# A hybrid RWKV-7, Mamba-2 and PEER step on one core: modulation products in two-part fp32r with 18 stationary columns, a halved last inverse level, weight splits ahead of stores, an unrolled TensorE program

## The reference, cut to what matters

```python
def _layer(x, c, shift0, wkv0, conv0, ssm0, lp):
    mod = jax.nn.silu(c) @ lp['w_ada'] + lp['b_ada']        # c: 9 conditioning rows; 6 x 1024 columns
    sh1, sc1, gt1, sh2, sc2, gt2 = jnp.split(mod, 6, axis=-1)
    xn = _rmsnorm(x, lp['norm1_g']) * (1 + sc1[:, None]) + sh1[:, None]
    proj = xn @ lp['w_in']                                  # 50 tiles of 128 columns, and 16 columns for dt
    p_rw, p_ssm, p_gate = ...
    o_a, wkvT = _rwkv7(p_rw, ...)                           # gate g, decay w, a: products of low rank, then the state
    o_b, convT, ssmT = _mamba2(p_ssm, ...)                  # x, B, C through a convolution of 4 taps and silu
    x = x + gt1[:, None] * (merged @ lp['w_out'])
    xn2 = _rmsnorm(x, lp['norm2_g']) * (1 + sc2[:, None]) + sh2[:, None]
    x = x + gt2[:, None] * _peer(xn2, ...)                  # 8 heads, top 16 of 128 x 128 experts per token
```

## Time and profile before

| | |
|---|---|
| median of 3 runs | 4652.97 us (4641.38 to 4659.5) |
| the profiled execution's own time | 4650.29 us |
| its span | 4648.5 us |
| PE busy | 4303.7 us (93%) |
| DVE busy | 3202.1 us (69%) |
| ACT busy | 1439.4 us (31%) |
| POOL busy | 1349.9 us (29%) |
| mean granted TensorE clock | 0.954 of full |

### The profile page before, as it was taken

One profiled execution on the slowest core, in us unless ns is written; L12 is line 12 of the kernel. 1 busy time (PEld: TensorE's weight loads), 2 busy tenths in 40 slices (PEclk: granted clock), 3 DMA queues, 4 the chain that ended last, 5 costly groups with the idle time before them and its releaser, 6 DMA issues. The chain is left out here.

```text
span 4648.5 us, 86226 instructions
## 1 busy us (share of the span) xinstructions
PE 4303.7 (93%) x32847; PEld 3863.9 (83%) x32847; DVE 3202.1 (69%) x6005; ACT 1439.4 (31%) x2182; POOL 1349.9 (29%) x1059
## 2 busy tenths in 40 slices
PE   6999998999767897999998999799999999999997
PEld 3888887777654786978887888799999999999997
DVE  4731332444384324889995555699999999999997
ACT  2211221111154322223335666322222222222223
POOL 5333222000002220024443222344344343434341
PEclk8999999999786998999999999899999999999999
DMA  4555555445262331124443455799999999999994
GB/s 158 184 185 191 187 191 181 171 162 204 74 190 78 106 122 56 37 68 144 143 143 135 162 180 183 273 303 303 299 302 299 302 300 300 300 299 305 297 302 165
DMA packets 522992, 927.81 MB, mean 200 GB/s; under 512 B 284032, under 2 KB 351232, under 8 KB 518688
## 3 DMA queue, kind: packets, MB, share of 16 engines
q1 hardware_dynamic: 380448, 547.61, 36.1%
q0 software_dynamic: 80960, 346.96, 21.9%
q10 hardware_dynamic: 61392, 30.52, 2.2%
HBM read 785.79 MB, written 206.30 MB: 213 GB/s over the span
## 5 line engine op out<-in xcount | busy, mean ns | idle before, releaser
L3188 POOL DMA_INDIRECT ex_rows<-expert_rows,ex_here x512 | 587.3, 1147 | 952.2 <-DVE acc_tok L3323 861.0
L3323 DVE SCALAR_TENSOR_TENSOR acc_tok<-ex_rows,ex_wsp,acc_tok 128x1024 f32<-128x1024 f32 x512 | 633.5, 1278 | 0.0
L2586 PE MATMUL ex_psa<-x_dense_high,eg_u_high 128*128 128x288 f32 x2048 | 604.4, 295 | 15.3 <-DVEq L3377 13.9
L2586 PE MATMUL ex_psa<-x_dense_low,eg_u_high 128*128 128x288 f32 x2048 | 604.6, 295 | 0.0
L2586 PE MATMUL ex_psa<-x_dense_high,eg_u_low 128*128 128x288 f32 x2048 | 604.2, 295 | 0.0
L2677 POOL TENSOR_TENSOR eg_u_low<-eg_u,eg_u_high 128x1024 fp32r<-128x1024 f32 x130 | 326.7, 2513 | 844.1 <-ACT eg_u_high L2672 844.1
L3220 PE MATMUL ex_pso<-ex_w_high,ex_v_high 128*128 128x288 f32 x2048 | 441.4, 297 | 8.9 <-DVE acc L3305 6.1
L3220 PE MATMUL ex_pso<-ex_w_high,ex_v_low 128*128 128x288 f32 x2048 | 440.1, 297 | 0.0
L3220 PE MATMUL ex_pso<-ex_w_low,ex_v_high 128*128 128x288 f32 x2048 | 439.1, 296 | 0.0
L3251 ACT ACTIVATE ex_w<-ex_psa 128x288 f32<-128x288 f32 x256 | 105.4, 412 | 1059.6 <-PE ex_psa L2586 1038.8
L3305 DVE TENSOR_TENSOR acc<-ex_pso,acc 128x576 f32<-128x576 f32 x512 | 373.7, 750 | 47.2 <-PE ex_pso L3220 47.2
(11 more groups left out here) (521 smaller groups left out, 9442.3 us busy)
## 6 DMA issues: line engine op xcount, KB each, us to landing
eg_u<-in_u SPq DMA_DIRECT2D x256, 512.0 KB, 3.7
expert_rows<-in_v SPq DMA_DIRECT2D x128, 512.0 KB, 6.1
ex_v<-in_v SPq DMA_DIRECT2D x128, 512.0 KB
weights<-wt_stage SPq DMA_DIRECT2D x9, 4096.0 KB, 12.1
ex_g<-weights SPq DMA_DIRECT2D x128, 288.0 KB
expert_rows<-eg_act SPq DMA_DIRECT2D x256, 128.0 KB, 1.7
proj<-in_out POOLq DMA_DIRECT2D x50, 548.5 KB, 3.3
in_w<-in_w_in SPq DMA_DIRECT2D x50, 512.0 KB, 3.6
```

What stands on the lines that cost most here:

```text
L2586: yield nc.tensor.matmul(out[:, 0:b - a], w[:, kc, :], half[:, kc, a:b], start=n == 0, stop=n == len(passes) - 1)
L3188: pool.indirect_dma_start(rows[i][:, :], None, table, index(here[par][:, t, j:j + 1]), element_offset=ROW_RUNS[t][0]).then_inc(s_row[i], 16)
L3323: v.scalar_tensor_tensor(out=acc_tok[:, t, :], in0=rows[i][:, at:at + D], scalar=wsp[:, i:i + 1], in1=acc_tok[:, t, :], op0=ALU.mult, op1= ...
```

## The change

It has six parts.

1. POOL splits the 16 dt columns of w_in first (`first_split`), and clears old semaphores (`clear_retired`) at the end of its program for the inputs.
2. In the inputs loop POOL waits for tile t's matmuls and splits the weights of tile t + 2; the store of tile t, which waits for the evacuation, comes behind.
3. In the four RWKV rounds the gate product and its copy come first, then zw, za, norm, bonus.
4. The last inverse level computes only the half that is used: PE leaves out one of the two matmuls, and DVE's `t` and `xy` are 128x256 in place of 128x512.
5. In rw_prompt POOL splits each 128x3072 chunk of w_ada (CAST, TENSOR_TENSOR), and the condition into 18 columns (high and low side by side). PE runs 16 fp32r matmuls in place of 8 of fp32; the row has 18 partitions, and the product that turns it adds its two halves (`fold`).
6. PE's program in spread is in line.

```diff
+    def first_split(self, pool):
+        pool.wait_ge(self.s_wdt, 16)
+        self.split(pool, self.wdt, self.wdth, self.wdtl, 0)
...
-                k.clear_retired()
+                pj.first_split(pool)
...
                 t = 2 * r + parity
+                pool.wait_ge(self.s_mm, t + 1)
+                split(t + 2, parity, r + 1)
                 store(t, parity)
-                split(t + 2, parity, r + 1)
...
-                            product(lw[0:64, r, 0, :], lora[0:64, 0, :], "zw")
+                            product(lw[:, r, 1, :], lora[:, 1, :], "gate")
                         elif j == 1:
+                            pe.wait_ge(AC.sem, AC.now("gate", r))
+                            product(lw[0:64, r, 0, :], lora[0:64, 0, :], "zw")
+                        elif j == 2:
                             pe.wait_ge(AC.sem, AC.now("sw", r))
                             product(lw[64:128, r, 0, :], lora[64:128, 0, :], "za")
-                        elif j == 2:
+                        elif j == 3:
                             pe.wait_ge(AC.sem, AC.now("a", r))
...
         for p_, rows in heads:
-            nc.tensor.matmul(pq[rows, p_, 0, :], ch.xy[rows, p_, 1, :], ch.mx[rows, p_, :], start=True, stop=True)
+            if lv < levels - 1:
+                nc.tensor.matmul(pq[rows, p_, 0, :], ch.xy[rows, p_, 1, :], ch.mx[rows, p_, :], start=True, stop=True)
...
-        v.tensor_tensor(xy, xy, tmp, ALU.subtract).then_inc(*DV.inc(f"xy{lv}_{h}"))
+        v.tensor_tensor(part(xy), part(xy), part(tmp), ALU.subtract).then_inc(*DV.inc(f"xy{lv}_{h}"))
...
+                for c in range(NCH):
+                    pool.wait_ge(s_wa[c % 2], 16 * (c // 2) + 16)
+                    g.tensor_copy(wah[c % 2][:, :, :], wa[c % 2][:, :, :]).then_inc(s_ah, 1)
+                    pool.wait_ge(s_ah, c + 1)
+                    g.tensor_tensor(wal[c % 2][:, :, :], wa[c % 2][:, :, :], wah[c % 2][:, :, :].bitcast(F32), ALU.subtract).then_inc(s_al, 1)
...
-                        rest = (nc.tensor.matmul(rowp, k.cT[:, kc, :], wa[h][:, kc, :], start=kc == 0, stop=kc == KC - 1)
-                                for kc in range(KC))
+                        rest = (nc.tensor.matmul(rowp, cond[:, kc, :], part[:, kc, :], start=kc == 0 and part is wah[h],
+                                                 stop=kc == KC - 1 and part is wal[h])
+                                for kc in range(KC) for part in (wah[h], wal[h]))
...
-                        pe.wait_ge(s_wa[h], 16 * r + 16)
+                        pe.wait_ge(s_al, 2 * r + h + 1)
+                        pe.wait_ge(s_cond, 3)
...
-                        for _ in range(4):
+                        for _ in range(KC):
                             next(rest)
...
-                blocks(pe, body)
+                in_line(body)
```

More of the change, by code:

```diff
@@ L533, in store @@
             pool.dma_start(io["proj"][t], self.out[parity][:, :]).then_inc(self.s_st[parity], 16)
-        pool.wait_ge(self.s_wdt, 16)
-        self.split(pool, self.wdt, self.wdth, self.wdtl, 0)
         one = pool.alloc_register("in_one")
@@ L617, in phase_inputs @@
         s_lora = k.sem("rwp_lora_step")
-        PE = Progress(k.sem("rwp_pe"), "zw", "za", "gate", "norm", "bonus")
-        AC = Progress(k.sem("rwp_act"), "sw", "a", "gate", "lam", "linv", "lprev", "ln", "rn")
+        PE = Progress(k.sem("rwp_pe"), "gate", "zw", "za", "norm", "bonus")
+        AC = Progress(k.sem("rwp_act"), "gate", "sw", "a", "lam", "linv", "lprev", "ln", "rn")
         DV = Progress(k.sem("rwp_dve"), "sub", "mix", "kkr", "sq", "cs", "csx", "norm_floor", "am", "kp", "kk",
@@ L684, in _ @@
                 pj.pool_side(pool)
+                k.clear_retired()
             @block.tensor
@@ L709, in pair_product @@
                             pe.wait_ge(DV.sem, DV.before("bonus", r))
+                            product(lw[:, r, 1, :], lora[:, 1, :], "gate")
+                        elif j == 1:
+                            pe.wait_ge(AC.sem, AC.now("gate", r))
                             product(lw[0:64, r, 0, :], lora[0:64, 0, :], "zw")
-                        elif j == 1:
+                        elif j == 2:
                             pe.wait_ge(AC.sem, AC.now("sw", r))
                             product(lw[64:128, r, 0, :], lora[64:128, 0, :], "za")
-                        elif j == 2:
+                        elif j == 3:
                             pe.wait_ge(AC.sem, AC.now("a", r))
-                            product(lw[:, r, 1, :], lora[:, 1, :], "gate")
-                        elif j == 3:
-                            pe.wait_ge(AC.sem, AC.now("gate", r))
                             pe.wait_ge(DV.sem, DV.now("sq", r))
@@ L805, in _ @@
                     evac(0)
+                    act.wait_ge(PE.sem, PE.now("gate", r))
+                    ac.activation(gate, pa[:, 0:T], ACT.Copy).then_inc(*AC.inc("gate"))
+                    evac(1)
                     act.wait_ge(s_w, 32)
@@ L809, in _ @@
                     ac.activation(sw, pa[:, 0:T], ACT.Sigmoid, bias=rp[:, bass.ds(8 * r + RWP_W0, 1)]).then_inc(*AC.inc("sw"))
-                    evac(1)
+                    evac(2)
                     act.wait_ge(PE.sem, PE.now("za", r))
                     ac.activation(a, pa[:, 0:T], ACT.Sigmoid, bias=rp[:, bass.ds(8 * r + RWP_A0, 1)]).then_inc(*AC.inc("a"))
-                    evac(2)
-                    act.wait_ge(PE.sem, PE.now("gate", r))
-                    ac.activation(gate, pa[:, 0:T], ACT.Copy).then_inc(*AC.inc("gate"))
                     act.wait_ge(DV.sem, DV.now("cs", r))
@@ L1106, in rw_matrix_dve @@
         at(PE, f"xmx{lv}_{h}")
+        needed = slice(0 if lv < levels - 1 else CL, 2 * CL)
+        part = lambda ap: ap[:, :, needed]
         lm = k.lv_mask[:, lv, :, :].rearrange("p i t -> p (i t)").unsqueeze(1)
-        v.tensor_tensor(tmp, pq, bc(lm, [P, NPAIR, 128]), ALU.mult).then_inc(*DV.inc(f"t{lv}_{h}"))
+        v.tensor_tensor(part(tmp), part(pq), bc(part(lm), [P, NPAIR, 2 * CL - needed.start]), ALU.mult).then_inc(*DV.inc(f"t{lv}_{h}"))
         at(DV, f"t{lv}_{h}")
-        v.tensor_tensor(xy, xy, tmp, ALU.subtract).then_inc(*DV.inc(f"xy{lv}_{h}"))
+        v.tensor_tensor(part(xy), part(xy), part(tmp), ALU.subtract).then_inc(*DV.inc(f"xy{lv}_{h}"))
         yield
@@ L1187, in phase_rw_prompt @@
         y = [sb(f"y{i}", [P, NPAIR, CL]) for i in range(2)]
-        wa = [sb(f"ada{i}", [P, KC, ADA_STEP * P]) for i in range(2)]
+        wa, wal = zip(*[(sb(f"ada{i}", [P, KC, ADA_STEP * P]), k.twin(f"rwc_ada_low{i}", [P, KC, ADA_STEP * P])) for i in range(2)])
+        wah = [ctx.enter_context(nc.sbuf_tensor(f"rwc_ada_high{i}", [P, KC, ADA_STEP * P], F32R)) for i in range(2)]
+        cond = ctx.enter_context(nc.sbuf_tensor("rwc_cond", [P, KC, 2 * NCOND], F32R))
+        fold = sb("fold", [2 * NCOND, NCOND])
         s_in = [k.s_first_chunk] + [k.sem(f"rwc_in{i}_loaded") for i in range(1, 4)]
@@ L1195, in phase_rw_prompt @@
         s_init = k.sem("rwc_state_zeroed")
+        s_cond = k.sem("rwc_cond_split")
+        s_ah = k.sem("rwc_ada_high_made")
+        s_al = k.sem("rwc_ada_low_made")
         heads = [(p_, rows) for p_ in range(NPAIR) for rows in halves()]
@@ L1198, in phase_rw_prompt @@
         ACOLS = ADA_STEP * P
-        row = sb("ada_row", [NCOND, ACOLS])
-        rowp = b.ps[0:NCOND, BANK_MOD, 0:ACOLS]
+        row = sb("ada_row", [2 * NCOND, ACOLS])
+        rowp = b.ps[0:2 * NCOND, BANK_MOD, 0:ACOLS]
         modp = b.ps[:, BANK_MOD, ACOLS:ACOLS + ADA_STEP * NCOND].rearrange("p (m c) -> p m c", m=ADA_STEP)
@@ L1256, in _ @@
             def _(pool):
-                k.clear_retired()
+                g = nc.gpsimd
+                g.tensor_copy(cond[:, :, 0:NCOND], k.cT[:, :, :]).then_inc(s_cond, 1)
+                g.tensor_tensor(fold[:, :], k.ident[0:2 * NCOND, 0:NCOND], k.ident[0:2 * NCOND, NCOND:2 * NCOND], ALU.add).then_inc(s_cond, 1)
+                pool.wait_ge(s_cond, 2)
+                g.tensor_tensor(cond[:, :, NCOND:2 * NCOND], k.cT[:, :, :], cond[:, :, 0:NCOND].bitcast(F32), ALU.subtract).then_inc(s_cond, 1)
+                for c in range(NCH):
[3 more added lines that the diff above has]
+                    g.tensor_tensor(wal[c % 2][:, :, :], wa[c % 2][:, :, :], wah[c % 2][:, :, :].bitcast(F32), ALU.subtract).then_inc(s_al, 1)
+                    if c == 1:
+                        k.clear_retired()
             @block.tensor
@@ L1316, in state_part @@
                         for m in range(ADA_STEP):
-                            mm = nc.tensor.matmul(modp[:, m, :], row[:, m * P:(m + 1) * P], k.ident[0:NCOND, 0:NCOND],
+                            mm = nc.tensor.matmul(modp[:, m, :], row[:, m * P:(m + 1) * P], fold[:, :],
                                                   start=True, stop=True)
```

## The result

The changed kernel takes 4672.27 us in the median of 13 runs (4660.84 to 4679.52), the kernel before 4650.25 in 13 runs beside them (4641.38 to 4662.55): +22.0 us, a ratio of 1.0045, 95% interval 1.0033 to 1.0056. So it is slower by an amount clear of the noise, and by the prediction's own bounds (4630 to 4676) it is still "same", to which it had given 0.24, against 0.58 for slower. The profiled execution took 4676.79 us, its span is 4675.0 in place of 4648.5: +26.5.

A forecast was written before the change was run, and what follows sets the result against it. PE's own work was taken to set the time in rw_prompt (busy 361.5 of 390 us). From 4650.3, −36 for the inputs phase and +72.5 for rw_prompt, nothing for spread, gave 4687 us; range 4625 to 4738.

The forecast's parts named there:

- The exclusion: DVE operations with two SBUF inputs and POOL instructions reading SBUF exclude each other for the whole instruction; without it 4563.
- PE's work: rw_prompt: sixteen fp32r products at 0.175 us each save 2.77 us per chunk, the halved last level 0.5 per chunk.
- A round: rw_prompt, two chunks: 45.9 us becomes 39.4, plus DVE-caused waits of 8.9 and 6.6, so 54.9, +9.0; seven rounds +63.
- the worst case: rw_prompt round at the worst alignment: each wait also brings a cold 2.0 us, so 58.9, +13.
- Waits and clock in the phase: rw_prompt: PE's savings against new waits give +72.5 us (+25 to +105); PE's waits for DVE some 100 us.
- The first matrix part: rw_prompt, chunks 0 and 1, no state part: two splits beside DVE and PE taking turns cost +15 us (10 to 18).
- The last round: rw_prompt's last round: only state parts and no split, so −5.5 us.
- The inputs phase: Before rw_prompt: earlier split −21, gate first −19, low-rank inputs' wait (L794) +3, first_split and clearing +1: −36 us (−12 to −45).
- Spread and the rest: Spread: its eight waits are for ACT's gating, already in line, so PE's in-line program changes nothing (±3 us).
- POOL doesn't bite: Rival in rw_prompt: DVE's operations slip in around splits or the exclusion fails; −51 there, 4563 us in all; chance 0.15.
- The splits land well: Rival in rw_prompt: well-aligned splits cost only +3.5 us per round, +29 there, 4643 in all; chance 0.25.
- The convolution's chain: Rival in the inputs: ACT's and DVE's chain still comes last, so the earlier split gives nothing; 4708 us; chance 0.1.

The follow-up runs named there:

- pieces8: The changed kernel with the split of each w_ada chunk in 8 pieces of 128x384, CAST and TENSOR_TENSOR in turn: 4567.66 us, ratio 0.9825.
- split_conv: The kernel before with only the split ahead of the store, for tiles 0 to 15 alone, while the convolution runs: 4617.45 us, ratio 0.9941.

## Why the prediction was right, point by point

The time, 4672, lies in the range, the direction is the forecast's, and the mechanism is the one that it named; the size was +22 of a forecast +36.5. Some of the terms are right by luck, as follows.

- **The exclusion.** Read from the earlier trace rows, right. `xy` under CAST and TENSOR_TENSOR, PE waiting at mt_1 and at mx3 of chunk 1: all four in the timeline above.
- **PE's work.** At full clock the new products start every 0.175 us, just as worked out from the dt product. The whole saving is smaller than the sum has it: in pieces8 PE is busy 40.6 us less than before (316.1 against 356.6), where the sum has 51.
- **A round.** 54.9 forecast; 56.1, 55.8, 56.0, 61.2, 51.6 and 57.2 measured, after one of 46.5, the first. Seven rounds: +63 forecast, +57.2 measured (the sum of the steps from rhs_0 to rhs_0, 384.3 against 327.1). The two waits of the round above were 4.1 and 6.4, with 1.4 and 0.8 beside them, 12.7 against 15.5; some three us more went into the clock, which I had left for the worst case. It was granted at half, the lower of its two levels, from 873.7 to 877.1, behind PE's wait of 4.1, and from 897.5 to 904.4, in and behind the wait of 6.4.
- **Waits and clock in the phase.** The sum has 51 us less work for PE and 123.5 of new waits (7 × 15.5 + 15). The trace has PE 16.4 less busy and 88.7 more idle. The waits were over-priced by some 35, and PE's busy time came out as much too high: 24 of it is the clock, by pieces8, where the same 7520 matmuls are 316.1 us and not 340.3, and 10 the smaller saving above. PE's waits for DVE, with 104.7 us, are near the 100 that it had written down as a sign.
- **The first matrix part.** +15 forecast, 30.6 to 44.9 us, +14.3.
- **The last round.** Forecast −5.5, "no split"; measured +0.9. This step failed: chunk 15's split lands at the start of that round (CAST at 1198.3), DVE's last `xy` takes 6.42 us, and PE waits 7.3 for rhs. That these errors, −5.8 and +6.4, cancel, and within the rounds waits and clock as well, makes +72.3 against +72.5 look better than it is.
- **The inputs phase.** −36 forecast, −42.2 measured, and 35.7 to 43.8 in the four kernels with the same code there. The parts were wrong. Part 2 has −21 in the sum; in the convolution alone it gives −26.0 (split_conv), but in the rounds it costs 26.9 by itself and 10.8 behind gate first, where the sum has +3 for the wait at L794 (which did grow, by 5.6). What the earlier split lets go on SP, a load and two copies, I did not count. Part 3 gives −24.7, −19 in the sum.
- **Spread and the rest.** I had them at nothing. The profiled execution has 3.6 us less outside the two phases, and the medians 4.5 less again than the profiled spans. Both are within the spread that phases with the same code show.
- **Rivals.** "POOL doesn't bite" gave 4563, and pieces8, in which it can't bite for long, runs at 4568. That is near in part by chance: its rw_prompt gained 36.4 us of the rival's 51, and 12 us came from phases behind it that it shares with the changed kernel. "The splits land well" did not occur in any round but the first. The convolution's chain did not come last: PE is busy all of 125 to 310.

## What to carry to other kernels

Before work is given to an idle POOL beside a busy DVE, look at what DVE's operations read: if both inputs are in SBUF and POOL reads SBUF too, the one that comes second waits for the other's whole instruction. So cut POOL's instructions down to about the slack of whoever waits for DVE, even if the sum of POOL's work grows. Here eight pieces, whose TENSOR_TENSOR takes 1.0 us, gave most, and four, at 1.9 us, could not be told from them. And when a step is moved ahead on a queue, follow what its end releases on other queues: here the split's gain was paid back in the rounds, where it let DMAs go earlier and ACT's stores landed later.

## What the runs showed of the hardware that was not expected

A MEMSET of 128x3072 on POOL takes 2.66 us, as long as the CAST (2.74), and 64 of them do not delay DVE at all, while the CAST does. And cutting POOL's instructions costs POOL time. A TENSOR_TENSOR takes 6.72 us for 3072 elements a partition and 1.0 for 384, a CAST 2.74 and 0.50, so that eight of each make 12.0 us and not 9.5. With what are probably waits for DVE (a CAST of 0.50 took up to 1.04), POOL is busy 13.1 us per chunk in pieces8 (209.7 / 16), where the two whole ones took 9.6 (153.7 / 16).
